# Loading an attention head with four DMAs where there were seven: duplicated q rows and stacked k rows in one transfer each

## The chip, the cores and the metric

The kernel runs on one core of a Trainium2 chip. The core has a matrix engine (TensorE, PE in the profile; its weight loads are PEld), a vector engine (VectorE, DVE), a scalar engine (ScalarE, ACT), a general engine (GpSimd, POOL) and a sequencer that mostly issues DMAs (SyncE, SP). Sixteen DMA engines move data between HBM and the on-chip SBUF, which has 128 partitions. Engines wait for each other by semaphores. A DMA adds 16 to its semaphore in all, once its data are there. The metric is device time in microseconds of one execution.

## The reference: one decoder layer

The input `x` is 2048 positions by 1024 features, float32. What is computed, cut to the lines that matter:

```python
h = rmsnorm(x, norm_mix_pre);  proj = h @ w_in          # 512 pool columns, then q, k, v: 512 each (8 heads of 64)
pool_out = multiscale_pool(proj[..., :512], w_pool)
# per head, query t, key s < t:
z = q @ k.T * 64**-0.5
stick = reverse_cumsum(log_sigmoid(-z)) - log_sigmoid(-z)
attn = exp(log_sigmoid(z) + stick) @ v                   # causal, strictly below the diagonal
x = x + rmsnorm(concat(rms(pool_out), rms(attn)) @ w_out)
x = x + rmsnorm((silu(gate) * val) @ w_down)             # gate, val = causal conv of (rmsnorm(x) @ w_up)
```

## The kernel before

The phases follow each other: values and transposed activations, projections, attention, the mixing stage with the output projection, the up projection with the convolution, and the down projection. Matrix products keep float32 accuracy by splitting each operand into a high and a low part of a shorter type, so q and k stand in HBM (`qk_scratch`) as a high and a low array of 128 rows for each pair of heads, 64 rows a head, 2048 columns.

In attention (`phase_attention`, line 531) a head is worked through in 40 units: 16 query blocks of 128 rows, and for each block its key chunks of up to 512 columns, from the diagonal backwards. Two heads make a pair, `e` is the head in the pair, and the four pairs run as one unrolled pair and a loop over the other three. A unit passes through all engines: PE makes the scores (`z_ps`, L806), ACT takes the two sigmoids (L680, L681), DVE scans (`stick`, L772), POOL multiplies (`weight`, L726), PE transposes (L823), ACT and DVE (L692, L689, L753) copy the transposed weights to SBUF, and PE multiplies them by v (L843, L833). Every engine works at a fixed lag behind the unit counter: the scores of unit u stand in PE's queue ahead of the values of unit u - 6. So when the scores of a new head's first unit wait, the values of the last six units of the head before wait behind them.

For a head the operands in SBUF are arranged on all 128 partitions: `k_both` holds k high on partitions 0 to 63 and k low on 64 to 127, `q_hi` holds q high twice (once on each half), and `q_lo` q low twice. There is one set of buffers for each `e`, so the load of a head can run only once the head two before has been worked through. What sets the order around the change is SP's queue:

- The first head is loaded in three parts, of 4, 4 and 8 tiles of 128 columns, each with its own semaphore (`head_parts`, L581). PE waits for part 1 before the first unit, for part 2 before query block 4, for part 3 before block 8 (L801). POOL waits for all three parts at once (L709), before it sums v high and v low (`v_f`, L712), and that stands ahead of the weights of query block 3.
- Then comes the whole load of the second head, and 16 loads of pieces of `w_out` (L659). From the third on these wait for POOL's work on the piece two before, which is spread over the second head's units.
- In the loop, for each head: a wait until PE is through with the values of that head (L662), the load of the head with the same `e` in the next pair, and the two stores of the finished head (`mixed`, L650, L651), behind a wait for its last output block.

Of the kernel before, what the change touches and what calls it, by code (L numbers as in the profile page):

```python
# [12 lines left out]
P = 128  # L13
# [4 lines left out]
HEAD_DIM = 64  # L18
# [8 lines left out]
def done(step, lead=LEAD):  # L27
    return step + 1 + lead


def freed(step, ring=LEAD, lead=LEAD):
    return step + 1 + lead - ring


def stored(uses, each=16):

    return each * uses + 16
# [21 lines left out]
def as_f32(tile):  # L59
    return tile.bitcast(F32)  # L60
# [470 lines left out]
def phase_attention(nc, a, c, s, wide, bridge):  # L531
# [8 lines left out]
    heads = a["d_attn"] // HEAD_DIM  # L540
# [18 lines left out]
    with ExitStack() as stack:  # L559
# [3 lines left out]
        q_hi = [n.sb(f"q_hi{i}", [P, seq], F32R) for i in range(2)]  # L563
        q_lo = [n.sb(f"q_lo{i}", [P, seq], F32R) for i in range(2)]
        k_both = [n.sb(f"k_both{i}", [P, seq], F32R) for i in range(2)]
# [13 lines left out]
        head_in, mixed_out = n.sems("head_in", 2), n.sems("mixed_out", 2)  # L579
# [6 lines left out]
            n.sem(x) for x in ("z_done", "rest_done", "beta_done", "stick_done", "weight_done",  # L586
                               "wT_turned", "wT_hi_done", "wT_whole_done", "wT_lo_done", "pv_done", "pv_whole_done", "o_read", "v_f_done"))

        pairs, loads = heads // 2, 7
        last_read = max(weight_lag, turn_lag, hi_lag, lo_lag, values_lag, read_lag)  # L590

        def steps(eng, step):

            def behind_of(i, u):
                def behind(lag):
                    v = u - lag
                    if v < 0 and isinstance(i, int) or v >= total:
                        return None  # L600

                    return (v, i * total + v) if v >= 0 else (v + total, i * total + v)
                return behind

            for u in range(total):
                step(0, u, behind_of(0, u))
            with eng.Fori(1, pairs) as i:
                for u in range(total):
                    step(i, u, behind_of(i, u))
            for u in range(total, total + last_read):  # L610
                step(pairs - 1, u, behind_of(pairs - 1, u))
# [9 lines left out]
        def col(q, key):  # L621

            return seq - (q + 1) * P + key

        def wo_part(i, u):

            m = (u - per_head) // 2
            return m if isinstance(i, int) and i == 0 and (u - per_head) % 2 == 0 and 0 <= m < 2 * a["kc"] else None

        with nc.Block() as block:  # L630

            @block.sync
            def _(sp):
                for sem in mixed_out:
                    sp.sem_inc(sem, 16)

                def load_head(pair, e, sem, first=0, end=tiles):

                    half, cols = slice(e * HEAD_DIM, (e + 1) * HEAD_DIM), slice(first * P, end * P)
                    for part in range(2):  # L640
                        rows = slice(part * HEAD_DIM, (part + 1) * HEAD_DIM)
                        sp.dma_start(as_f32(k_both[e][rows, cols]), s["qk"][pair + heads // 2, part, half, cols]).then_inc(sem, 16)
                        for hi_lo, dst in enumerate((q_hi, q_lo)):
                            sp.dma_start(as_f32(dst[e][rows, cols]), s["qk"][pair, hi_lo, half, cols]).then_inc(sem, 16)
                    sp.dma_start(as_f32(v_both[e][:, first:end, :, :]), s["v"][pair * 2 + e][:, first:end, :, :]).then_inc(sem, 16)

                def store_head(pair, e):
                    sp.wait_ge(o_read, done((pair * 2 + e + 1) * tiles - 1, lead))
                    row = (pair * 2 + e) * HEAD_DIM
                    sp.dma_start(s["merged"][bass.ds(a["d_pool"] + row, HEAD_DIM), :], mixed[e][0:HEAD_DIM, :]).then_inc(mixed_out[e], 16)  # L650
                    sp.dma_start(s["attn_low"][bass.ds(row, HEAD_DIM), :], mixed[e][HEAD_DIM:P, :]).then_inc(mixed_out[e], 16)  # L651

                for first, end, sem in head_parts:
                    load_head(0, 0, sem, first, end)
                load_head(0, 1, head_in[1])
                for m in range(2 * a["kc"]):
                    if m >= 2:
                        sp.wait_ge(wo_done, m - 1)
                    sp.dma_start(wo_f[:, m % 2, :], wo_rows[m // 2][:, (m % 2) * BANK:(m % 2 + 1) * BANK]).then_inc(wo_in[m % 2], 16)  # L659
                with sp.Fori(0, heads // 2 - 1) as i:  # L660
                    for e in range(2):
                        sp.wait_ge(pv_whole_done, i * per_pair_whole + (whole_before[(e + 1) * per_head] + lead))  # L662
                        load_head(i + 1, e, head_in[e])
                        store_head(i, e)
                for e in range(2):
                    store_head(heads // 2 - 1, e)
                for e in range(2):
                    sp.wait_ge(mixed_out[e], stored(heads // 2, 32))
# [27 lines left out]
            @block.gpsimd  # L696
            def _(pool):
                pool.sem_inc(weight_done, lead)

                def low_wo(m):  # L700
                    k, h = m // 2, m % 2
                    pool.wait_ge(wo_hi_done, m + 1)
                    pool.tensor_tensor(wide[2 + h][:, k, :], wo_f[:, h, :], as_f32(wide[h][:, k, :]), ALU.subtract).then_inc(wo_done, 1)

                def sum_v(pair, e):

                    if isinstance(pair, int) and pair == 0 and e == 0:
                        for _, _, sem in head_parts:
                            pool.wait_ge(sem, 16 * loads)  # L709
                    else:  # L710
                        pool.wait_ge(head_in[e], 16 * loads * pair + 16 * loads)
                    pool.tensor_tensor(v_f[e][:, :, :], as_f32(v_both[e][:, :, 0, :]), as_f32(v_both[e][:, :, 1, :]), ALU.add).then_inc(v_f_done, 1)  # L712

                def step(i, u, behind):
                    if wo_part(i, u) is not None:
                        low_wo(wo_part(i, u))
                    if behind(weight_lag):
                        v, t = behind(weight_lag)
                        e, q, key, w, first, _ = units[v]
                        if v in v_sum_at:  # L720
                            sum_v(i if u >= weight_lag else i - 1, v_sum_at[v])
                        pool.wait_ge(beta_done, done(t, lead))
                        pool.wait_ge(stick_done, done(t, lead))
                        pool.wait_ge(turned, freed(t, weight_ring, lead))
                        at = col(q, key) + 1
                        pool.tensor_tensor(weight[v % weight_ring][:, 0:w], beta[v % stick_in][:, 0:w], stick[q % 2][:, at:at + w],  # L726
                                           ALU.mult).then_inc(weight_done, 1)

                steps(pool, step)
# [62 lines left out]
            def _(pe):  # L792
# [3 lines left out]
                def scores(i, u):  # L796
                    e, q, key, w, first, _ = units[u]
                    if isinstance(i, int) and i == 0 and e == 0:
                        for start, _, sem in head_parts:
                            if first and q == start:  # L800
                                pe.wait_ge(sem, 16 * loads)  # L801
                    elif u % per_head == 0:
                        pe.wait_ge(head_in[e], 16 * loads * i + 16 * loads)
                    pe.wait_ge(stick_done, freed(i * total + u, z_ring, lead))
                    for k, half in enumerate((q_hi, q_lo)):
                        m = pe.matmul(z_ps[u % z_ring][:, 0:w], half[e][:, q * P:(q + 1) * P], k_both[e][:, key:key + w],  # L806
                                      start=(k == 0), stop=(k == 1))
                        if first and k == 0:
                            pe.matmul(z_ps[u % z_ring][:, w - P:w], c["ident_r"][:, :], c["not_before"][:, :], start=False, stop=False)
                    m.then_inc(z_done, 1)  # L810
# [678 lines left out]
def build(nc, a, out):  # L1489
# [20 lines left out]
    with ExitStack() as stack:  # L1510
# [21 lines left out]

        wide = [n.sb(f"wide{i}", [P, a["kc"], BANK], F32R) for i in range(4)]
        phase_attention(nc, a, c, s, wide, bridge)

        up_start = {"h": [n.sb(f"up_start_h{i}", [P, a["kc"], BANK], F32R) for i in range(2)],
# [30 lines left out]
```

## Time and profile before

| | us |
|---|---|
| Time, median of 3 runs (lowest, highest) | 2728.99 (2728.14, 2729.57) |
| The profiled execution's own time | 2729.57 |
| Its span in the trace | 2727.9 |
| PE busy, share of the span | 2551.4, 94% |
| PE's waits for DMAs in the attention stage | 17.4 in 3 waits |
| POOL's wait for the first head's v | 11.0 in 1 wait |

How to read it: the span runs from the first to the last recorded instruction, and 1.7 us of the execution lie outside it. A row of a timeline gives start and length in microseconds, engine, line, operation, and in brackets how long the engine stood idle before and what ended that. A row of the view by windows gives for each engine its busy time in a stretch and its number of instructions, then the granted clock of PE as a share of 2.4 GHz, the mean busy share of the 16 DMA engines (a little over 1 where packets of one engine overlap), and the rate in GB/s. In the DMA view a row is a kind of transfer: how many, how large, and the median time from issue to landing.

### The profile page before, as it was taken

Reading aid. Unit: us, or ns where it says so; the run is one execution under the profiler, and the core shown is the slowest. Engines: PE = TensorE matmul, PEld = TensorE weight load, DVE = VectorE, ACT = ScalarE, POOL = GpSimd, SP = SyncE. Lnnn points to the kernel's source line nnn. Section 1 sums busy time; section 2 is a strip of 40 time slices with the busy share of each in tenths; the row PEclk is TensorE's granted clock in tenths of the full one; section 3 lists DMA queues with packets and bytes.
Section 4 is the critical chain, followed back from the end, with each engine's and each line's share of the span. In section 5 each row is a group of like instructions: output and inputs, shape, how many; then the busy total and the mean of one; then the engine's idle time right before and its main releaser. Section 6 shows DMA issues by size and latency. Waiting matters only on the chain. (4 is left out here: it accounts for less than half of the span.)

```text
span 2727.9 us, 37244 instructions
## 1 busy us (share of the span) xinstructions
PE 2551.4 (94%) x12453; PEld 2095.9 (77%) x12453; DVE 1340.3 (49%) x1748; ACT 1074.1 (39%) x1828; POOL 452.0 (17%) x416
## 2 busy tenths in 40 slices
PE   6989996999999979978999999999999989999997
PEld 5767885778777868757888888888888878787776
DVE  4434223999898957862343333334333333434432
ACT  4311113788887845542222222223222222333322
POOL 0000002776665622220000000000000000101001
PEclk9999997999999989988999999999999999999998
DMA  8922336163333036787111111111111144545453
GB/s 236 285 61 85 126 114 161 34 169 86 79 78 79 17 93 204 218 261 253 42 54 42 54 38 56 46 48 54 42 54 38 47 143 144 191 142 189 145 192 112
DMA packets 248429, 307.96 MB, mean 113 GB/s; under 512 B 11589, under 2 KB 176125, under 8 KB 243709
## 3 DMA queue, kind: packets, MB, share of 16 engines
q1 hardware_dynamic: 243708, 289.81, 34.9%
q0 software_dynamic: 4608, 16.78, 1.5%
q8 instruction: 55, 0.90, 0.1%
q14 instruction: 58, 0.47, 0.1%
HBM read 195.39 MB, written 94.37 MB: 106 GB/s over the span
## 5 line engine op out<-in xcount | busy, mean ns | idle before, releaser
L726 POOL TENSOR_TENSOR weight<-beta,stick 128x512 f32<-128x512 f32 (+3 forms) x320 | 304.9, 959 | 613.9 <-ACT beta L680 449.9
L1288 DVE SCALAR_TENSOR_TENSOR conv<-value_ps,taps,conv 128x512 f32<-128x512 f32 (+2 forms) x176 | 131.2, 746 | 370.6 <-ACT conv L1248 370.6
L1391 POOL TENSOR_TENSOR y<-y,x 128x1024 f32<-128x1024 f32 x16 | 38.9, 2433 | 1448.8 <-DVE y L1450 1448.5
L772 DVE TENSOR_TENSOR_SCAN stick<-z_ps,stick,beta 128x512 f32<-128x512 f32 x192 | 245.4, 1278 | 31.3 <-ACT z_ps L681 30.6
L506 PE MATMUL out_ps<-hT,w_hi 128*128 128x512 f32 x768 | 239.8, 393 | 9.9 <-DVE w_lo L440 9.9
L1248 ACT ACTIVATE conv<-value_ps,taps 128x512 f32<-128x512 f32 x88 | 68.7, 781 | 390.7 <-PE value_ps L1314 390.7
L1314 PE MATMUL gate_ps<-wide,wu_hi 128*128 128x512 f32 x704 | 218.1, 391 | 2.4 <-DMA wide<-h2T_scratch 2.4
L1314 PE MATMUL value_ps<-wide,wu_hi 128*128 128x512 f32 x704 | 216.8, 389 | 0.0
L1288 DVE SCALAR_TENSOR_TENSOR conv<-gate_ps,taps,conv 128x512 f32<-128x512 f32 (+2 forms) x176 | 131.1, 745 | 172.1 <-ACT conv L1248 172.1
L680 ACT ACTIVATE beta<-z_ps 128x512 f32<-128x512 f32 (+3 forms) x320 | 170.7, 533 | 95.0 <-PE z_ps L806 77.2
L823 PE MATMUL wT_ps<-ident,weight 128*128 128x128 f32 x1088 | 177.5, 279 | 28.3 <-DVE wT L753 15.2
L823 PEld LDWEIGHTS wT_ps<-ident,weight 128*128 128x128 f32 x1088 | 132.2, 141 | 73.7 <-DVE wT L753 26.2
L506 PEld LDWEIGHTS out_ps<-hT,w_hi 128*128 128x128 f32 x768 | 145.1, 189 | 42.3 <-DVE w_lo L440 10.3
L681 ACT ACTIVATE z_ps<-z_ps 128x512 f32<-128x512 f32 (+3 forms) x320 | 171.1, 535 | 0.0
L1314 PEld LDWEIGHTS gate_ps<-wide,wu_hi 128*128 128x128 f32 x704 | 133.0, 189 | 30.5 <-issue 2.8
L1314 PEld LDWEIGHTS value_ps<-wide,wu_hi 128*128 128x128 f32 x704 | 132.0, 188 | 27.4
L806 PE MATMUL z_ps<-k_both,q_hi 128*128 128x512 f32 (+3 forms) x320 | 131.1, 410 | 22.3 <-DMA v_both<-v_scratch 17.4
L506 PE MATMUL out_ps<-hT,w_lo 128*128 128x512 f32 x384 | 150.2, 391 | 0.0
L1248 ACT ACTIVATE conv<-gate_ps,taps 128x512 f32<-128x512 f32 x88 | 68.5, 778 | 186.3 <-PE gate_ps L1314 186.3
L833 PE MATMUL o_ps<-wT_f,v_f 128*64 128x128 f32 x1024 | 139.5, 279 | 0.0
L1314 PE MATMUL gate_ps<-wide,wu_lo 128*128 128x512 f32 x352 | 137.4, 390 | 0.0
L1314 PE MATMUL value_ps<-wide,wu_lo 128*128 128x512 f32 x352 | 136.9, 389 | 0.0
(168 smaller groups left out, 5400.9 us busy)
## 6 DMA issues: line engine op xcount, KB each, us to landing
wu_f<-in_w_up SPq DMA_DIRECT2D x44, 512.0 KB, 5.6
f_scratch<-f SPq DMA_DIRECT2D x88, 256.0 KB, 2.4
bridge<-in_w_down SPq DMA_DIRECT2D x44, 512.0 KB, 3.4
bridge<-f_scratch SPq DMA_DIRECT2D x88, 256.0 KB, 3.7
wd_f<-in_w_down SPq DMA_DIRECT2D x44, 512.0 KB, 3.6
xt<-in_x SPq DMA_DIRECT2D x16, 512.0 KB, 5.8
hT<-h_hi SPq DMA_DIRECT2D x16, 512.0 KB, 4.6
hT<-h_lo SPq DMA_DIRECT2D x16, 512.0 KB, 5.5
```

Source lines behind the costliest of these rows:

```text
L506: m = pe.matmul(out_ps[half + j][:, :], w[slot][:, k, :], hT[h][:, k, j * BANK:(j + 1) * BANK], start=(k == 0 and t == 0), stop=(k == kc - ...
L680: act.activation(beta[u % stick_in][:, 0:w], z_ps[u % z_ring][:, 0:w], ACT.Sigmoid, scale=scale).then_inc(beta_done, 1)
L681: act.activation(z_ps[u % z_ring][:, 0:w], z_ps[u % z_ring][:, 0:w], ACT.Sigmoid, scale=-scale).then_inc(rest_done, 1)
L726: pool.tensor_tensor(weight[v % weight_ring][:, 0:w], beta[v % stick_in][:, 0:w], stick[q % 2][:, at:at + w], ALU.mult).then_inc(weight_do ...
L772: dve.tensor_tensor_scan(stick[q % 2][:, at:at + w][:, ::-1], backwards, beta[u % stick_in][:, 0:w], start, ALU.mult, ALU.bypass).then_inc ...
L806: m = pe.matmul(z_ps[u % z_ring][:, 0:w], half[e][:, q * P:(q + 1) * P], k_both[e][:, key:key + w], start=(k == 0), stop=(k == 1))
L823: m = pe.transpose(wT_ps[u % wT_ring][:, b * P:(b + 1) * P], weight[u % weight_ring][:, b * P:(b + 1) * P], c["ident"][:, :])
L833: m = pe.matmul(o_ps[q % 2][0:HEAD_DIM, 0, :], v_f[e][:, key // P + b, :], wT_f[whole_before[u] % wT_ring][:, b, :], start=False, stop=Fal ...
L1248: act.activation(conv[g % 2][h][:, :], ps[h][:, g * BANK:(g + 1) * BANK], ACT.Identity, scale=column(3, h, slot), bias=column(0, h, slot)) ...
L1288: dve.scalar_tensor_tensor(out=out, in0=ps[h][:, g * BANK - back + skip:(g + 1) * BANK - back], scalar=column(kind, h, slot), in1=out, op0 ...
L1314: m = pe.matmul(ps[h][:, g * BANK:(g + 1) * BANK], w[slot][:, h, k, :], hT[x][g][:, k, :], start=(k == 0 and t == 0), stop=(k == kc - 1 an ...
L1391: pool.tensor_tensor(y[t][:, :], y[t][:, :], x2[t][:, :], ALU.add).then_inc(added, 1)
```

## The change

The load of a head is written with three DMAs in place of six for q and k. For q, a source with a leading dimension of two and a step of zero reads the same 64 rows twice, and the destination is all 128 partitions. For k, the source's leading dimension of two steps from the high to the low array. The order changes too: q high, q low, k, v. A head's semaphore thus gets 4 x 16 and no longer 7 x 16, and the waits of PE and POOL count accordingly.

```diff
-        pairs, loads = heads // 2, 7
+        pairs = heads // 2
...
-                    for part in range(2):
-                        rows = slice(part * HEAD_DIM, (part + 1) * HEAD_DIM)
-                        sp.dma_start(as_f32(k_both[e][rows, cols]), s["qk"][pair + heads // 2, part, half, cols]).then_inc(sem, 16)
-                        for hi_lo, dst in enumerate((q_hi, q_lo)):
-                            sp.dma_start(as_f32(dst[e][rows, cols]), s["qk"][pair, hi_lo, half, cols]).then_inc(sem, 16)
+                    for hi_lo, dst in enumerate((q_hi, q_lo)):
+                        twice = s["qk"][pair, hi_lo, half, cols].unsqueeze(0).broadcast_to([2, HEAD_DIM, (end - first) * P])
+                        sp.dma_start(as_f32(dst[e][:, cols]), twice).then_inc(sem, 16)
+                    sp.dma_start(as_f32(k_both[e][:, cols]), s["qk"][pair + heads // 2, :, half, cols]).then_inc(sem, 16)
                     sp.dma_start(as_f32(v_both[e][:, first:end, :, :]), s["v"][pair * 2 + e][:, first:end, :, :]).then_inc(sem, 16)
...
-                            pool.wait_ge(sem, 16 * loads)
+                            pool.wait_ge(sem, 16 * 4)
...
-                                pe.wait_ge(sem, 16 * loads)
+                                pe.wait_ge(sem, 16 * 4)
```

The compiled instructions give each access as a list of (step, count). For part 1 the destination of a q load is [128 partitions], [1], [512 columns] and its source [step 0, count 2], [step 2048, count 64], [512]; for k the source is [step 262144, count 2], [step 2048, count 64], [512]. Before, both sides of each were [64], [512]. The v load is [128], [512] on both sides, before and after.

On SP, at the start of attention, these are the loads of part 3 of the first head before (the numbers are partitions x elements):

```order
L642 DMA k_both<-qk_scratch 64x1024
L644 DMA q_hi<-qk_scratch 64x1024
L644 DMA q_lo<-qk_scratch 64x1024
L642 DMA k_both<-qk_scratch 64x1024
L644 DMA q_hi<-qk_scratch 64x1024
L644 DMA q_lo<-qk_scratch 64x1024
L645 DMA v_both<-v_scratch 128x1024
```

And the same place now, with the second head's load behind it:

```order
L642 DMA q_hi<-qk_scratch 128x1x1024
L642 DMA q_lo<-qk_scratch 128x1x1024
L643 DMA k_both<-qk_scratch 128x1x1024
L644 DMA v_both<-v_scratch 128x1024
L642 DMA q_hi<-qk_scratch 128x1x2048
L642 DMA q_lo<-qk_scratch 128x1x2048
L643 DMA k_both<-qk_scratch 128x1x2048
L644 DMA v_both<-v_scratch 128x2048
```

Ahead of the loop there are 28 loads before and 16 now; v moves from the seventh to the fourth place of each group.

On SP, inside the loop, before (an ISA row is an instruction that prepares an address or waits):

```order
L642 ISA
L642 DMA k_both<-qk_scratch 64x2048
L644 ISA
L644 DMA q_hi<-qk_scratch 64x2048
L644 ISA
L644 DMA q_lo<-qk_scratch 64x2048
L642 ISA
L642 DMA k_both<-qk_scratch 64x2048
L644 DMA q_hi<-qk_scratch 64x2048
L644 DMA q_lo<-qk_scratch 64x2048
L645 ISA
L645 DMA v_both<-v_scratch 128x2048
```

And now, with the wait and the first store behind it:

```order
L642 ISA
L642 DMA q_hi<-qk_scratch 128x1x2048
L642 ISA
L642 DMA q_lo<-qk_scratch 128x1x2048
L643 ISA
L643 DMA k_both<-qk_scratch 128x1x2048
L644 ISA
L644 DMA v_both<-v_scratch 128x2048
L647 ISA
L649 ISA
L649 DMA merged_scratch<-mixed 64x2048
```

The stores of the finished head stand right behind v as before. PE, ACT, DVE and POOL keep their order.

## Rows read from the trace of the kernel before

**Rows 1.** The page: span, busy time, and share of the DMA engines.
```profile
span 2727.9 us, 37244 instructions
...
PE 2551.4 (94%) x12453; PEld 2095.9 (77%) x12453; DVE 1340.3 (49%) x1748; ACT 1074.1 (39%) x1828; POOL 452.0 (17%) x416
```

**Rows 2.** Waits in the attention stage, 428 to 990 us.
```profile
PE z_ps L806 <- DMA v_both<-v_scratch: 17.4, 3, 13.5
POOL v_f L712 <- DMA v_both<-v_scratch: 11.0, 1, 11.0
```

**Rows 3.** PE's timeline: attention's start, first scores of heads 2, 3, 4, 8.
```profile
436.47 0.48 PE L806 MATMUL z_ps<-k_both,q_hi 128*128 128x128 f32 x1 [13.46 <-DMA v_both<-v_scratch]
...
456.33 1.11 PE L823 MATMUL wT_ps<-ident,weight 128*128 128x128 f32 x4 [9.68 <-POOL weight L726]
...
509.71 0.33 PE L806 MATMUL z_ps<-k_both,q_hi 128*128 128x128 f32 x1
...
583.62 0.32 PE L806 MATMUL z_ps<-k_both,q_hi 128*128 128x128 f32 x1 [1.43 <-DMA v_both<-v_scratch]
...
647.77 0.33 PE L806 MATMUL z_ps<-k_both,q_hi 128*128 128x128 f32 x1
...
911.21 0.33 PE L806 MATMUL z_ps<-k_both,q_hi 128*128 128x128 f32 x1
```

**Rows 4.** POOL's timeline at the first head.
```profile
452.88 2.34 POOL L712 TENSOR_TENSOR v_f<-v_both 128x1024 f32<-128x1024 f32 x1 [11.01 <-DMA v_both<-v_scratch]
```

**Rows 5.** SP's timeline: loads of heads 1, 3 and 5 (first and last issue).
```profile
428.35 0.59 SPq L642 DMA_DIRECT2D k_both<-qk_scratch  x1
...
432.41 0.59 SPq L645 DMA_DIRECT2D v_both<-v_scratch  x1
...
441.09 0.59 SPq L645 DMA_DIRECT2D v_both<-v_scratch  x1
...
562.15 0.51 SPq L642 DMA_DIRECT2D k_both<-qk_scratch  x1
...
657.71 0.52 SPq L642 DMA_DIRECT2D k_both<-qk_scratch  x1
```

**Rows 6.** By windows: the start of loading, one head's load, the last head on.
```profile
428.00:430.00 2.00, 0.00 (x0) 0.00 (x0) 0.09 (x2) 1.28 (x1) 0.00 (x0) 0.50 0.04 13
430.00:432.00 2.00, 0.00 (x0) 0.00 (x0) 0.00 (x0) 0.00 (x0) 0.00 (x0) 0.50 0.52 178
436.00:440.00 4.00, 3.53 (x12) 2.97 (x12) 1.20 (x3) 1.98 (x6) 0.74 (x2) 0.51 0.85 218
647.80:657.70 9.90, 9.90 (x75) 8.59 (x75) 7.13 (x12) 7.67 (x19) 6.97 (x7) 1.00 0.00 1
662.00:670.00 8.00, 7.07 (x50) 5.91 (x50) 7.78 (x14) 6.72 (x15) 5.51 (x6) 1.00 1.02 208
677.00:678.00 1.00, 1.00 (x8) 0.93 (x8) 1.00 (x2) 0.75 (x2) 0.71 (x2) 1.00 1.01 426
911.20:2727.90 1816.70, 1723.81 (x7781) 1422.74 (x7780) 790.84 (x954) 597.37 (x838) 150.46 (x107) 0.98 0.34 110
```

**Rows 7.** DMA view, 655 to 725 us: packets of nine DMAs.
```profile
DMA packets 802, 5.45 MB, mean 78 GB/s; under 512 B 144, under 2 KB 144, under 8 KB 144
```

**Rows 8.** DMA view of the whole execution: packets, and five kinds of its 727 issues.
```profile
DMA packets 248429, 307.96 MB, mean 113 GB/s; under 512 B 11589, under 2 KB 176125, under 8 KB 243709
...
k_both<-qk_scratch SPq DMA_DIRECT2D x4, 128.0 KB, 3.4
...
rows<-in_conv_w SPq DMA_DIRECT2D x3, 22.0 KB
rows<-in_conv_b SPq DMA_DIRECT2D x1, 22.0 KB
rows<-in_pool_scale SPq DMA_DIRECT2D x1, 2.0 KB
rows<-in_attn_scale SPq DMA_DIRECT2D x1, 2.0 KB
```

More of the change, by code:

```diff
@@ L708, in sum_v @@
                         for _, _, sem in head_parts:
-                            pool.wait_ge(sem, 16 * loads)
+                            pool.wait_ge(sem, 16 * 4)
                     else:
-                        pool.wait_ge(head_in[e], 16 * loads * pair + 16 * loads)
+                        pool.wait_ge(head_in[e], 16 * 4 * pair + 16 * 4)
                     pool.tensor_tensor(v_f[e][:, :, :], as_f32(v_both[e][:, :, 0, :]), as_f32(v_both[e][:, :, 1, :]), ALU.add).then_inc(v_f_done, 1)
@@ L800, in scores @@
                             if first and q == start:
-                                pe.wait_ge(sem, 16 * loads)
+                                pe.wait_ge(sem, 16 * 4)
                     elif u % per_head == 0:
-                        pe.wait_ge(head_in[e], 16 * loads * i + 16 * loads)
+                        pe.wait_ge(head_in[e], 16 * 4 * i + 16 * 4)
                     pe.wait_ge(stick_done, freed(i * total + u, z_ring, lead))
```

## The prediction, on record before the changed kernel ran

> **What bounds the kernel now.** I read the page first. PE is busy for 94% of the span [rows 1], so time is lost where PE stands still, and a change in SP's queue matters only where PE or what feeds it waits for a transfer. The loads in question run in the attention stage, so I then read the waits of that stage: PE waited for loads 17.4 us in three waits, POOL 11.0 us in one [rows 2]. The timelines place them. PE's first scores come at 436.47 after an idle of 13.46 us, most of it before the loads are even issued. PE stops again for 9.68 us, to 456.33, because POOL stands until 452.88 for all three parts of head 1 [rows 3, 4]. Head 3 waits 1.43 us for its load [rows 3]. Elsewhere the loads are hidden. What hides them is a slack that can be read: the load that is issued 9.9 us into head 4 (657.71 against 647.77) [rows 3, 5] is for head 5. A head lasts 64.2 us (583.62 to 647.77) [rows 3], so a load has some 54 us from its issue.
>
> **How fast a load runs, and why.** The windows show one head's load [rows 6]. While the six 64-partition transfers run, the sixteen engines move 208 GB/s at a share of 1.02, 12.7 GB/s each. At the end, when v (128 partitions) and the stores run, they move 426 GB/s at 1.01, 26.4 GB/s each. So an engine can do 26.4, and the 64-partition transfers got half of it with all sixteen at work. The Trainium skill, "SBUF — State Buffer", section "Door 1: The DMA port swizzle", says that partitions 0 to 63 reach only 8 of the 16 ports; the trace agrees, with 208 against 426 GB/s. This speaks for the change: its q and k transfers span all 128 partitions.
>
> What speaks against it is the number of engines. A DMA leaves small packets on the engines it uses: nine DMAs of 64 or 128 partitions in 655 to 725 us left 144, sixteen each [rows 7]. Over the whole execution 727 issues would leave 11632, but there are 11589 [rows 8]. The 43 missing fit, to one packet, transfers spread over a divisor of their row count: four transfers of 44 rows (22 KB in rows of 512 bytes) on 11 engines miss 20, two of 4 rows on 4 engines miss 24. So a short outer dimension costs engines here. The changed q and k loads have 2 as the outer dimension of the source and 128 as that of the destination. No transfer of before has unequal ones, so the trace does not say which counts: 2, then two engines carry all of q and k; or 128, then sixteen do. A divisor must suit both sides for each engine to have a whole share, so I take 2. The Trainium skill, "DMA: Bandwidth & Descriptors", section "Rules for kernel authors", says that a leading zero-stride broadcast of c copies confines the whole DMA to at most c engines; the trace agrees as far as the 43 packets go, and by that rule the time comes out as forecast below.
>
> **The change part by part.** Removed: 3 of 7 issues a load, 0.6 us each on SP [rows 5]. Their gain is at most 1.9 us, and only where v is awaited from issue: at the start. It vanishes if two engines carry the data. The new order (v fourth) and the wait counts cost nothing by themselves: v still lands last, behind 192 rows on the two engines. Changed: the distribution. An engine of the two gets 64 rows from each of three DMAs and its usual 8 of v, 200 rows. At 8 KB that is 1.638 MB, at 26.4 GB/s 62.1 us a head; 31.0 us for part 3 (4 KB rows) and 15.5 us for part 1 or 2 (2 KB rows). Fixed times: bytes start about 1.5 us after the first issue (428.35; 13 GB/s in 428 to 430, 178 after) [rows 5, 6]. A 128 KB load lands in 3.4 us [rows 8], of which 0.7 is data at 178 GB/s [rows 6], so about 1.0 is left behind the last byte. Bounds for the rate: 12.7 and 26.4 GB/s an engine. I take 26.4, since two engines that write to different partition halves are nearer to v's row than to the crowded one. All issues go into one queue in order, so each load starts when the one before is through.
>
> - Part 1: bytes from 429.9 to 445.4, PE starts at 446.4, not 436.47.
> - Part 2 ends at 460.9, part 3 at 491.9. POOL is released at 492.9, not 452.88: 40.0 us later. Head 1 is worked through from there as before, so head 2 could start at 509.71 + 40.0 = 549.7.
> - Head 2's load: 491.9 + 62.1 + 1.0 = 555.0. Head 2 starts there, 45.3 us late.
> - Head 3's load is issued behind the pieces of w_out, which POOL paces in head 2: 562.15 + 45.3 = 607.5 [rows 5]. It takes 1.5 + 62.1 + 1.0 = 64.6 us. Head 3 starts at 672.1, not 583.62: 88.5 us late.
> - From here a load is late every time. It is issued 9.9 us after the start of the head before, because the values of the last six units of the head before that stand behind the new head's scores in PE's queue, and SP waits for them. So a head cannot begin sooner than 9.9 + 64.6 = 74.5 us after the last. Those 9.9 us are all PE work (9.90 busy) [rows 6], at a granted clock of 1.00. After an idle of this kind the granted clock was 0.51 over the 4 us of 436 to 440 [rows 6], the lower of the two levels, 1.2 GHz. I add 1.7 us for it (bounds 0, and 4 if it lasts 8 us): 76.2 us a head.
> - Head 8 starts at 672.1 + 5 x 76.2 = 1053.1. What follows took 1816.7 us and has no such load in it [rows 6]. Span 2869.8. With the 1.7 us that lie outside the span (2729.57 against 2727.9), 2871.5, so 142 us more than the profiled execution, which itself is 0.6 us above the median.
>
> What is late next: nothing behind head 8, since no load is issued after head 6's values. The stores go behind v on the same queue and are over before the next load's issue. POOL's other waits for v (one a head) are released by the same load as PE.
>
> **Rivals.** 1. Sixteen engines, all 128 partitions. Then a head's 4.19 MB runs at 426 GB/s in 9.8 us instead of 17.6 (3.15 MB at 208, 1.05 at 426) [rows 6]. At the start v of part 1 is issued fourth, three issues of 0.7 us sooner (the step from 428.35 to 432.41 is six issues) [rows 5]: PE starts 2.0 us sooner. v of part 3 is the twelfth issue, at about 428.35 + 11 x 0.63 = 435.3 and not 441.09; data up to it end at 429.9 + 9.8 = 439.7, so POOL is free at 441 and its weights come before PE asks. The 9.68 us and the 1.43 us of head 3 go [rows 3]: 2.0 + 9.7 + 1.4 = 13.1 us, 2716. For it: the destination has 128. Against it: the divisor must suit 2. It decides as soon as the outer dimension of 2 does not limit the engines. This is the rival on the other side, and faster.
> 2. Two engines at 12.7 GB/s, half rate. Part 2 ends at 494.4, part 3 at 558.9, head 2 starts at 688.9, head 3 at 562.15 + 179.2 + 131.5 = 872.9 (129.0 us of data, 2.5 fixed), and the period is 143.1 us: 872.9 + 715.5 + 1816.7 + 1.7 = 3407. For it: that rate did stand in the trace for this source. Against it: it came with sixteen engines on 64 partitions.
> 3. Two engines, but hidden from head 3 on, if they do over 30 GB/s each or the load is issued earlier: only the 88.5 us stay, 2818. Against it: 62 us of data do not fit into 54, and 426 GB/s was the highest steady rate.
> 4. Nothing but fewer issues (the transfers stay as they are, and the 9.68 us too): 2 us less, 2727, no change that counts.
>
> **Numbers.** Forecast, two engines at full rate: 0.80. Rival 1: 0.11. Rival 2: 0.05. Rival 3: 0.03. Rival 4: 0.01. Within the forecast the clock term can take off 8.5 us or add 11.5, the fixed times are uncertain by 1 us a load, and a queue that one engine holds back may cost some per cent of the rate (2 us a load, 14 in all) or hold SP. So 2850 to 2910 is its own range; 2840 to 2930 with a little of the rest, and it leaves out the rivals, 2 in 10. The predicted time is that of the forecast, 2871. A measurement of this kernel can tell about 0.2% from no change, 5.5 us: faster 0.11, same 0.02, slower 0.87.
>
> **What would show it.** Small packets (under 512 B) fall from 11589 by 60 x 16 = 960 and rise by 30 x 2 = 60 with two engines, to 10689, or by 480 with sixteen, to 11109. During a load the rate should be about 53 GB/s at a DMA share of 0.12 over more than 60 us. PE's first scores should start at 446, POOL's `v_f` at 493, and PE should wait for a load at the start of head 3 for some 45 us (672.1 less 555.0 and the 72.5 us that head 2 takes without its wait of 1.43), and of heads 4 to 8 for about 10 us each, with heads 76 us apart. The forecast is wrong if the landings of q and k stay under 20 us.

## The result and the profile after

The changed kernel took 2900.26 us (median of 4 runs, 2899.41 to 2902.09) against 2729.28 us: a ratio of 1.0628, with a 95% interval of 1.0609 to 1.0646. It is 171 us slower; 142 were forecast.

Page of the changed kernel, against [rows 1] and [rows 8]:

```profile
span 2897.5 us, 37190 instructions
PE 2560.0 (88%) x12453; PEld 2104.3 (73%) x12453; DVE 1341.1 (46%) x1748; ACT 1074.5 (37%) x1828; POOL 451.7 (16%) x416
...
DMA packets 247528, 307.95 MB, mean 106 GB/s; under 512 B 10688, under 2 KB 175224, under 8 KB 242808
```

PE's busy time is almost as before, 2560.0 us; the rest is idle. The small packets are 10688, against 10689 expected for two engines and 11109 for sixteen: thirty transfers leave two packets each, to within one.

PE's timeline (start, length, engine, line, operation, idle before and its end), the first scores of heads 1, 2, 3, 4 and 8, against [rows 3]. The line numbers are one lower than before:

```profile
447.46 0.47 PE L805 MATMUL z_ps<-k_both,q_hi 128*128 128x128 f32 x1 [24.75 <-DMA v_both<-v_scratch]
...
561.76 0.48 PE L805 MATMUL z_ps<-k_both,q_hi 128*128 128x128 f32 x1 [8.69 <-DMA v_both<-v_scratch]
...
680.69 0.47 PE L805 MATMUL z_ps<-k_both,q_hi 128*128 128x128 f32 x1 [46.95 <-DMA v_both<-v_scratch]
...
759.86 0.47 PE L805 MATMUL z_ps<-k_both,q_hi 128*128 128x128 f32 x1 [13.05 <-DMA v_both<-v_scratch]
...
1080.18 0.47 PE L805 MATMUL z_ps<-k_both,q_hi 128*128 128x128 f32 x1 [13.35 <-DMA v_both<-v_scratch]
```

Every head now begins with a wait for its load. From head 3 to head 8 there are 399.5 us, 79.9 a head, where before a head took 64 to 67. POOL's wait, against [rows 4]:

```profile
495.94 2.34 POOL L711 TENSOR_TENSOR v_f<-v_both 128x1024 f32<-128x1024 f32 x1 [43.08 <-DMA v_both<-v_scratch]
```

The windows of the changed kernel (stretch, length, busy time of PE, PEld, DVE, ACT, POOL, granted clock, DMA share, GB/s), against [rows 6]:

```profile
447.00:451.00 4.00, 3.54 (x12) 2.96 (x12) 1.21 (x3) 1.98 (x6) 0.75 (x2) 0.50 0.13 50
681.00:692.50 11.50, 11.50 (x75) 10.06 (x74) 5.90 (x10) 7.31 (x18) 4.82 (x5) 0.83 0.02 8
700.00:725.00 25.00, 24.77 (x173) 20.34 (x172) 23.44 (x34) 21.61 (x49) 15.37 (x16) 1.00 0.13 54
731.00:737.00 6.00, 6.00 (x43) 4.82 (x41) 5.61 (x8) 5.69 (x12) 4.05 (x4) 1.00 0.92 244
745.00:758.00 13.00, 1.80 (x14) 1.31 (x12) 3.10 (x4) 2.22 (x5) 3.13 (x3) 0.68 0.13 53
1080.30:2897.50 1817.20, 1724.41 (x7780) 1423.32 (x7780) 789.53 (x952) 596.92 (x837) 148.24 (x105) 0.97 0.34 110
```

A load now runs at 54 GB/s with a DMA share of 0.13, which is two engines of sixteen at 27 GB/s each. Only from 731 to about 740 do the others work, for v and the stores; the row shows the first six of these nine microseconds. While PE waits (745 to 758) it is busy for 1.80 of 13 us. What follows head 8 takes 1817.2 us, as the 1816.7 of before. So the whole loss lies in attention.

SP's timeline of one load, against [rows 5]:

```profile
692.45 0.61 SPq L642 DMA_DIRECT2D q_hi<-qk_scratch  x1
693.26 0.58 SPq L642 DMA_DIRECT2D q_lo<-qk_scratch  x1
694.03 16.36 SPq L643 DMA_DIRECT2D k_both<-qk_scratch  x1
710.60 20.10 SPq L644 DMA_DIRECT2D v_both<-v_scratch  x1
731.02 0.57 SPq L649 DMA_DIRECT2D merged_scratch<-mixed  x1
```

The issue of k takes 16.36 us and that of v 20.10, where an issue took 0.6. A likely reason, not tested by itself, is that the queue of the two engines is full and SP stands until there is room. So v and the stores are moved in the middle of the load. The forecast had put v's rows last on the two engines, but gave the crowding in the middle no price.

### The profile page after: what moved, and what is told of

Its sections match the earlier page's. It is cut to its first block and busy times, and to the rows that moved or that the text cites. A ratio compares the mean times of both kernels' runs of the same rounds, so it can differ in the third digit from the quotient of the medians.

```text
span 2897.5 us, 37190 instructions
## 1 busy us (share of the span) xinstructions
PE 2560.0 (88%) x12453; PEld 2104.3 (73%) x12453; DVE 1341.1 (46%) x1748; ACT 1074.5 (37%) x1828; POOL 451.7 (16%) x416
## 2 busy tenths in 40 slices
DMA packets 247528, 307.95 MB, mean 106 GB/s; under 512 B 10688, under 2 KB 175224, under 8 KB 242808
## 5 line engine op out<-in xcount | busy, mean ns | idle before, releaser
L805 PEld LDWEIGHTS z_ps<-k_both,q_hi 128*128 128x128 f32 x320 | 63.1, 197 | 183.8 <-issue 130.6
L771 DVE TENSOR_TENSOR_SCAN stick<-z_ps,beta 128x128 f32<-128x128 f32 (+3 forms) x128 | 104.5, 816 | 198.4 <-ACT z_ps L680 166.2
```

What stands on the lines that cost most here:

```text
L771: dve.tensor_tensor_scan(stick[q % 2][:, at:at + w][:, ::-1], backwards, beta[u % stick_in][:, 0:w], start, ALU.mult, ALU.bypass).then_inc ...
```

## The experiments

**The same loads, with the long dimension outermost.** All sums over the 128 partitions are the same if q and k share another order of rows, so row r and its copy can stand on partitions 2r and 2r + 1.

```diff
-                        twice = s["qk"][pair, hi_lo, half, cols].unsqueeze(0).broadcast_to([2, HEAD_DIM, (end - first) * P])
+                        twice = s["qk"][pair, hi_lo, half, cols].unsqueeze(1).broadcast_to([HEAD_DIM, 2, (end - first) * P])
...
-                    sp.dma_start(as_f32(k_both[e][:, cols]), s["qk"][pair + heads // 2, :, half, cols]).then_inc(sem, 16)
+                    sp.dma_start(as_f32(k_both[e][:, cols]), s["qk"][pair + heads // 2, :, half, cols].rearrange("t r n -> r t n")).then_inc(sem, 16)
```

> The same four loads a head, the same bytes and the same number of issues as the changed kernel, but the source lists its 64 rows outermost and the two copies (step 0) or the two arrays (high, low) inside: partition 2r and 2r+1 belong to row r for q and for k alike, so the scores are the same sums in another order. Theory A (the short outermost dimension of the source puts a load on two engines): small packets rise to 11589 - 960 + 480 = 11109, the loads run at over 400 GB/s, PE starts near 434.5, v_f of head 1 starts near 441, and the time is 2716 (2712 to 2722), 13 us below before and 184 below the changed kernel. Theory B (what costs is that a source has two rows of destinations per row, or that one DMA has 128 descriptors, or the order with v last): the time stays near 2900.

Measured: 2720.08 us (6 runs), ratio 0.9969 (0.9957 to 0.9981). Its page, a window inside a load, PE's wait behind POOL, and POOL's row:

```profile
DMA packets 247947, 307.94 MB, mean 113 GB/s; under 512 B 11108, under 2 KB 175644, under 8 KB 243228
```

```profile
651.00:656.00 5.00, 4.57 (x32) 3.87 (x33) 4.96 (x9) 4.04 (x10) 2.99 (x4) 1.00 1.00 405
```

```profile
445.92 1.11 PE L822 MATMUL wT_ps<-ident,weight 128*128 128x128 f32 x4 [3.67 <-POOL weight L725]
```

```profile
442.48 2.34 POOL L711 TENSOR_TENSOR v_f<-v_both 128x1024 f32<-128x1024 f32 x1 [3.35 <-DMA v_both<-v_scratch]
```

The small packets are 11108: sixteen engines. The load runs at 405 GB/s, and the time is 180 us below the changed kernel, with the same number of DMAs, bytes and rows per DMA. Theory B is out: neither the repeated read, nor the number of rows in a DMA, nor v in the last place costs the 171 us. The gain over before is 9.0 and 9.6 us in the medians of two series, less than the 13 expected. POOL is released at 442.48, not 452.88, but 3.67 us of PE's wait of 9.68 are left. On the other side the expectation had left out a wait of PE for part 2 of head 1, which stands in the trace of before and is gone now:

```profile
442.54 0.33 PE L806 MATMUL z_ps<-k_both,q_hi 128*128 128x128 f32 x1 [2.50 <-DMA v_both<-v_scratch]
```

The profiled run itself took 2716.37, 13.2 us less than the profiled run of before. Its timeline accounts for 12.7 of them: PE starts 2.75 us sooner, 6.01 us of the wait for POOL are gone, and so are the waits of 2.50 and 1.43.

**The order alone.** The seven loads, q high, q low, k, v.

```diff
+                    for hi_lo, dst in enumerate((q_hi, q_lo)):
+                        for part in range(2):
+                            rows = slice(part * HEAD_DIM, (part + 1) * HEAD_DIM)
+                            sp.dma_start(as_f32(dst[e][rows, cols]), s["qk"][pair, hi_lo, half, cols]).then_inc(sem, 16)
...
```

> The seven loads of before, only in the changed kernel's order (q high twice, q low twice, k high and low, v). Theory A: no load uses fewer engines, so 11589 small packets and 2729 (2727 to 2731). If the order had a part in the loss, some of the 171 us shows here.

Measured: 2725.46 us (10 runs), ratio 0.9991 (0.9982 to 1.0001), no change that counts, though the median lies 1.5 us below the expected range. Small packets 11588. The order has no part in the loss.

**One of the three loads back on sixteen engines.**

```diff
-                    for hi_lo, dst in enumerate((q_hi, q_lo)):
-                        twice = s["qk"][pair, hi_lo, half, cols].unsqueeze(0).broadcast_to([2, HEAD_DIM, (end - first) * P])
-                        sp.dma_start(as_f32(dst[e][:, cols]), twice).then_inc(sem, 16)
+                    twice = s["qk"][pair, 0, half, cols].unsqueeze(0).broadcast_to([2, HEAD_DIM, (end - first) * P])
+                    sp.dma_start(as_f32(q_hi[e][:, cols]), twice).then_inc(sem, 16)
+                    for part in range(2):
+                        rows = slice(part * HEAD_DIM, (part + 1) * HEAD_DIM)
+                        sp.dma_start(as_f32(q_lo[e][rows, cols]), s["qk"][pair, 1, half, cols]).then_inc(sem, 16)
```

> The changed kernel with q low loaded by two 64-partition loads again (five DMAs a head); q high and k stay as changed. Theory A: 64 + 64 + 8 + 8 rows on each of the two engines, about 46 us a head. That is under the slack of 54 us, so from head 4 on nothing waits and heads are 64 to 67 us apart again; left are a start of head 1 at 443, v_f at 477 (24 late), and head 3 at 632 (48 late): 2778 (2770 to 2790). Small packets 11589 - 960 + 10 x (2 + 2 + 16 + 16) = 10989. A rival in which each confined DMA costs a fixed sum (its issue held up on SP) expects two thirds of the 171 us: 2843.

Measured: 2791.91 us (4 runs), ratio 1.0227 (1.0211 to 1.0242), so 63 us over before. Its page and PE's first scores of heads 3 and 4:

```profile
DMA packets 247828, 307.94 MB, mean 110 GB/s; under 512 B 10989, under 2 KB 175525, under 8 KB 243109
```

```profile
643.48 0.47 PE L807 MATMUL z_ps<-k_both,q_hi 128*128 128x128 f32 x1 [32.08 <-DMA v_both<-v_scratch]
...
709.37 0.33 PE L807 MATMUL z_ps<-k_both,q_hi 128*128 128x128 f32 x1
```

The packets are 10989, as expected: the stacked k and the doubled q each run on two engines, so the step of zero is not needed for it. Head 3 still waits 32.08 us, head 4 not at all, and 65.9 us lie between them. Taking one of the three transfers off the two engines (144 rows each in place of 200) takes away 108 of the 171 us, not 57: what counts is whether a load fits into the slack of some 54 us, and not a fixed price per DMA. The time is 14 us above the expectation, and head 3 came at 643, not at 632. Its load was issued at 591.38 and took 52.1 us to the scores, where 144 rows at 26.4 GB/s and the fixed 2.5 us make 47.2: the load on the two engines again took longer than its bytes.

**v first.**

```diff
+                    sp.dma_start(as_f32(v_both[e][:, first:end, :, :]), s["v"][pair * 2 + e][:, first:end, :, :]).then_inc(sem, 16)
                     for hi_lo, dst in enumerate((q_hi, q_lo)):
...
```

> The changed kernel with v issued ahead of q and k. In the changed kernel SP is held for 16 and 20 us at the issue of k and v, and v's rows on the other fourteen engines and the two stores then run for about 12 us together with the two busy engines, while a head's load takes 67.6 us from first issue to the scores and not the forecast 64.6. If v and the stores crowding in cost these 3 us, v first takes away v's part: heads 78 to 79 us apart instead of 80, time 2888 to 2896. If the loss comes from the stores alone, or if it is something in the two engines, it stays at 2900 within 3.

Measured: 2890.21 us (4 runs), ratio 1.0590 (1.0574 to 1.0607): 10 us less than the changed kernel. PE's and SP's timelines of the load of head 4:

```profile
679.48 0.47 PE L805 MATMUL z_ps<-k_both,q_hi 128*128 128x128 f32 x1 [44.87 <-DMA k_both<-qk_scratch]
...
756.23 0.47 PE L805 MATMUL z_ps<-k_both,q_hi 128*128 128x128 f32 x1 [10.90 <-DMA k_both<-qk_scratch]
```

```profile
690.98 0.35 SPq L640 DMA_DIRECT2D v_both<-v_scratch  x1
```

From the first issue to the scores this load takes 65.3 us (690.98 to 756.23), against 67.4 in the changed kernel (692.45 to 759.86). Heads 3 to 8 are 78.0 us apart on average (head 8 begins at 1069.41), against 79.9. So 2 of the 3 us a load beyond the forecast come with v's transfer in the middle. The stores still fall into the load, and what they cost was not measured apart. (The stretch in which all engines worked in the changed kernel's load was 9 us long, 731 to 740, not 12.)

**q and k issued once they are free.**

```diff
-                        sp.wait_ge(pv_whole_done, i * per_pair_whole + (whole_before[(e + 1) * per_head] + lead))
-                        load_head(i + 1, e, head_in[e])
+                        sp.wait_ge(z_done, i * total + ((e + 1) * per_head + lead))
+                        load_head(i + 1, e, head_in[e], v_after=...)   # the wait of before stands ahead of v alone
```

> The changed kernel, with q and k of the next pair's head issued once the scores of the head in work are done (they alone read q and k), and only v behind the wait for its values. The loads stay on two engines. Theory: the period of 80 us is 11.5 us of waiting for the values (they stand behind the stalled scores in PE's queue) and 67.6 us of load; with the early issue the loads follow each other back to back, so a head takes what its load takes, 66 to 69 us, near to the 64 to 67 us of its own work. Head 3 stays at 681, head 8 comes at 681 + 5 x 67 = 1016 instead of 1080.5: 2836 (2825 to 2850). Rival: the 11.5 us are not a part of the period but PE's slow restart, and the time stays within 10 us of 2900.

Measured: 2838.66 us (4 runs), ratio 1.0408 (1.0392 to 1.0424): 62 us less than the changed kernel, with the loads still on two engines. PE's waits in attention:

```profile
PE z_ps L808 <- DMA v_both<-v_scratch: 99.8, 8, 46.1
```

In the changed kernel this row is:

```profile
PE z_ps L805 <- DMA v_both<-v_scratch: 161.1, 9, 46.9
```

Heads 3 to 8 are 66 to 70 us apart. The first 11.5 us of head 3:

```profile
679.70:691.20 11.50, 11.50 (x68) 10.23 (x69) 5.60 (x9) 6.49 (x17) 3.95 (x4) 0.77 0.13 54
```

PE restarts here at a low clock too (0.77), but a load runs beside it at 54 GB/s, where in the changed kernel 8 GB/s moved at this place. So the time in which a load waited for the values was part of the period. The lower clock after the stall is a small part of that time: in the changed kernel the same number of PE's instructions (75) took 11.5 us, against 9.9 before.

**A faster version.** On top of the interleaved loads, POOL sums head 1's v in two parts (`sum_part` adds v high and v low of a range of tiles).

```diff
-                        for _, _, sem in head_parts:
+                        for _, _, sem in head_parts[0:2]:
                             pool.wait_ge(sem, 16 * 4)
+                        sum_part(0, 2 * per)
+                        return
...
+                        if isinstance(i, int) and i == 0 and v == rest_at and u < total:
+                            pool.wait_ge(head_parts[2][2], 16 * 4)
+                            sum_part(2 * per, tiles)
...
-                        pe.wait_ge(v_f_done, 2 * i + (e + 1))
+                        pe.wait_ge(v_f_done, 1 if isinstance(i, int) and i == 0 and e == 0 and key < 2 * per * P else 2 * i + (e + 2))
```

> The interleaved loads (all sixteen engines), and POOL sums head 1's v in two parts: tiles 0 to 7 once parts 1 and 2 have landed, tiles 8 to 15 ahead of the weights of query block 7. In the interleaved kernel PE still waits 3.67 us at 446 for POOL, which waited 3.35 us for part 3. Theory: that wait goes and nothing takes its place: 3 us less than the interleaved kernel beside it. Rival: POOL's second sum of 1.2 us and the earlier weights only move the wait, since at that point DVE's scans and PE at the low clock pace the stage: within 1 us of it.

> The interleaved kernel once more, for a comparison with the split sum on the same chip and for the size of its gain: a ratio of 0.995 to 0.998 to before.

Measured beside each other: the split sum 2712.91 us (5 runs), ratio 0.9947 (0.9934 to 0.9961); the interleaved loads alone 2718.32 us (5 runs), ratio 0.9965 (0.9952 to 0.9979). POOL and PE of the split sum:

```profile
440.28 1.28 POOL L706 TENSOR_TENSOR v_f<-v_both 128x512 f32<-128x512 f32 x1
...
450.59 1.27 POOL L706 TENSOR_TENSOR v_f<-v_both 128x512 f32<-128x512 f32 x1
```

```profile
443.50 0.63 PE L831 MATMUL wT_ps<-ident,weight 128*128 128x128 f32 x4 [0.21 <-DVE wT L761]
```

Neither of POOL's sums waits, and PE's wait at this point is 0.21 us. The split gives 5.4 us in the medians, where 3 were expected; the wait of PE for POOL at this place was 4.32 us in the interleaved kernel run beside it, and the rest is not explained. The intervals overlap, so the size is not settled. This version beats both kernels, by 15 us (0.5%) and 187 us.

## Why the prediction was right, and what was mis-sized

- **Two engines, by the shorter outer dimension.** Right: 10688 small packets, one off the forecast, and 54 GB/s. The interleaved source shows that it is the place of the short dimension that decides. Both rules of the Trainium skill that the prediction weighed held. With the rule of the Trainium skill in "SBUF — State Buffer", section "Door 1: The DMA port swizzle", the trace agrees: a load on sixteen engines over all 128 partitions ran at 405 GB/s instead of 208. With the rule of the Trainium skill in "DMA: Bandwidth & Descriptors", section "Rules for kernel authors", it agrees too: the source with two copies outermost was confined to two engines, by the 10688 small packets.
- **Start.** PE began at 447.46 (forecast 446.4), POOL at 495.94 (492.9), head 2 at 561.76 (555.0), head 3 at 680.69 (672.1). The prediction's path is the one taken. Two readings of the start were off and changed nothing in the forecast: of PE's 13.46 us of idle only 5.3 lie before the first issue (423.01 to 428.35), not most, and the third of the three waits, 2.50 us at 442.54, was not placed.
- **The period.** 79.9 us, forecast 76.2. Its first term, the values behind the stalled scores with the clock, was right: 11.8 us (680.69 to 692.45) against 9.9 + 1.7, and 11.9 on average over the five periods. The 1.7 for the clock was given with bounds but no working, so that it fits so well is in part luck. The granted clock of that stretch was 0.83, against 1.00 before. The early issue showed that this term is real. The waits of heads 4 to 8 were 13.0 to 14.4 us, where about 10 were named, and that of head 3 46.95 (some 45).
- **The term that was too small** is the load: 64.6 us in the forecast, 67.4 to 68.8 measured for heads 4 to 8. The rate of 26.4 GB/s an engine holds while the two are alone with rows of 8 KB (54 GB/s), but not from first to last byte. The prediction had named a queue that holds back, 2 us a load, as an uncertainty and not in its sum. It was 3 to 4: v and the stores ran in the middle, beside q and k. From 732 to 739 the mean packet of 8 KB took 475 ns over all engines, against 311 ns in 700 to 725, and v first took 2 of the 3 us away; the rest was not measured apart. For head 1 the rows are shorter, and there the rate itself was lower: in the changed kernel's trace a packet of 2 KB took 84 ns (24.4 GB/s) and one of 4 KB 159 ns (25.8), which makes POOL's 3 us. Over the loads of heads 1 to 8, one behind another, the longer loads are about 25 of the 27 us by which head 8 came late (1080.18 against 1053.1), and the first term of the period the other 2. These 27 us are nearly all of the 29 that the forecast missed.
- **Rivals.** Half rate would have shown 25 GB/s; hidden loads would have shown no waits from head 4 on, which is what the load with one transfer fewer on the two engines showed. Sixteen engines was priced at 2716, and the interleaved kernel, which is that case, took 2720 and 2718. Its price counted all of the 9.68 us as gone and left out the 2.50.
- **The sign of being wrong.** Landings of q and k under 20 us can't be read: the DMA view gives no landing for them in the changed kernel. The 67.4 us from first issue to scores stand in their place.

## What to carry to other kernels

Look at the outermost dimension of both sides of a DMA, not only at its bytes and its number of partitions: 2 outermost (in the source here; a short destination was not tried) puts it on two engines, and the count of small packets (2 or 16 a transfer) shows it at once. If a copy or a stack of two is wanted, put the two inside the long dimension and let the other operand follow the same order. A load that is hidden has a slack counted from the moment it can be issued, and once it is late, what is queued behind the stalled instruction adds to every period.

## What the hardware showed unexpectedly

SP itself stood for 16.36 and 20.10 us at the issue of one DMA, with 64 rows of 8 KB for each of the two engines per transfer; in two of the six loads in the loop the issue of k took 1.5 to 1.9 us and that of v 36 to 37. At the start, with rows of 2 KB, four of the eight issues took 5.0 to 7.7 us. With sixteen engines (the interleaved kernel) an issue took 0.4 to 0.7 us. That the queue of the two engines was full is the likely reason, argued from these times. A transfer that uses all engines (v) is then started late too, and the load is longer while it runs: 2 us, by the run with v first.
